# A two-layer block on one core: the gate rows spread by one fp32r product over high and low parts, and the first level of a block inverse built by VectorE's transpose on four quarters

## What is computed

```python
gc = jnp.cumsum(g, -1)
diff = gc[..., :, None] - gc[..., None, :]
decay = jnp.where(lower, jnp.exp(jnp.where(lower, diff, 0.0)), 0.0)
kb = k * beta[..., None]
L = jnp.where(strict, jnp.einsum('bhnid,bhnjd->bhnij', kb, k) * decay, 0.0)
rhs = jnp.concatenate([v * beta[..., None], kb * jnp.exp(gc)[..., None]], -1)
sol = lax.linalg.triangular_solve(L + jnp.eye(C, dtype=L.dtype), rhs, left_side=True,
                                  lower=True, unit_diagonal=True)
u, w = sol[..., :dv], sol[..., dv:]
```

## Time and profile before

| what | value |
|---|---|
| median of 3 runs | 2718.54 us (2718.34 to 2718.98) |
| profiled execution, span from first to last instruction | 2717.0 us |
| TensorE busy | 2678.4 us, 99% of the span |
| VectorE busy | 1909.8 us, 70% |
| ScalarE busy | 1212.6 us, 45% |
| GpSimd busy | 854.2 us, 31% |
| mean granted TensorE clock | 0.996 of full speed |

### The profile page before, as it was taken

The page is one execution under the profiler, slowest core; times in us unless marked ns, Lnnn a source line. Parts: engine busy times, 40 slices in busy tenths (PEclk is TensorE's granted clock), DMA queues, the critical chain, the costliest instruction groups (busy, mean ns, idle before and its releaser), DMA issues.

```text
span 2717.0 us, 45293 instructions
## 1 busy us (share of the span) xinstructions
PE 2678.4 (99%) x17387; PEld 2250.4 (83%) x17387; DVE 1909.8 (70%) x2190; ACT 1212.6 (45%) x1572; POOL 854.2 (31%) x646
## 2 busy tenths in 40 slices
PE   6999999999999999999999999999999999999998
PEld 4798998899898888888888888889777778888887
DVE  1476777787787687666666666588999997655554
ACT  2355455545546445333333333354433334444344
POOL 1076676676667412600000000004565550000000
PEclk9999999999999999999999999999999999999999
DMA  9966666676665676666666666655555556666664
GB/s 364 354 219 207 227 225 204 223 239 200 224 229 188 219 223 228 189 187 186 187 190 188 190 186 186 185 162 172 171 179 170 161 173 187 192 186 186 192 202 155
DMA packets 283976, 552.53 MB, mean 203 GB/s; under 512 B 16882, under 2 KB 54323, under 8 KB 282675
## 3 DMA queue, kind: packets, MB, share of 16 engines
q1 hardware_dynamic: 263488, 473.49, 56.5%
q0 software_dynamic: 19472, 76.06, 7.4%
q10 hardware_dynamic: 866, 0.80, 0.1%
HBM read 548.19 MB, written 2.10 MB: 203 GB/s over the span
## 4 chain that ended last, share of the span: by engine, by line
PE 96%; DMA 2%; DVE 1%; SPq 1%; ACT 0%; issue 0%; DVEq 0%
PE pg L1220 40%; PE pd L1220 18%; PE pg L936 13%; PE pg L923 6%; PE pg L1207 4%; PE pg L955 3%; PE pd L849 2%; DMA wr<-in_gdn_w_in 1%; PE pd L1096 1%; PE pd L1078 1%; PE pd L1415 1%; PE pd L1428 1%; DMA arena<-in_mod_w 1%; PE pg L849 1%; PE pd L1027 1%; PE pd L1010 1%
## 5 line engine op out<-in xcount | busy, mean ns | idle before, releaser
L2341 DVE TENSOR_TENSOR wl<-wr,wh 128x1024 fp32r<-128x1024 f32 x615 | 773.7, 1268 | 453.7 <-ACT wh L1818 451.2
L1818 ACT ACTIVATE wh<-wr 128x1024 fp32r<-128x1024 f32 x616 | 652.8, 1061 | 936.2 <-PE pg L1220 590.3
L662 POOL TENSOR_TENSOR wl<-wr,wh 128x1024 fp32r<-128x1024 f32 x195 | 478.9, 2458 | 366.3 <-ACT wh L1599 231.3
L1220 PE MATMUL pg<-wh,hh 128*128 128x512 f32 x1344 | 529.8, 394 | 0.3 <-DVE hl L2414 0.3
L1220 PE MATMUL pg<-wl,hh 128*128 128x512 f32 x1344 | 527.3, 392 | 0.0
L1220 PE MATMUL pg<-wh,hl 128*128 128x512 f32 x1344 | 525.7, 391 | 0.0
L1599 ACT ACTIVATE wh<-wr 128x1024 fp32r<-128x1024 f32 x216 | 227.7, 1057 | 356.4 <-PE pg L936 196.4
L1220 PEld LDWEIGHTS pg<-wh,hh 128*128 128x128 f32 x1344 | 252.6, 188 | 59.1 <-DVE wl L2341 2.4
L936 PE MATMUL pg<-hh,wh 128*128 128x256 f32 x1024 | 300.7, 294 | 0.8 <-ACT arena L1659 0.8
L1220 PEld LDWEIGHTS pg<-wh,hl 128*128 128x128 f32 x1344 | 252.5, 188 | 56.3
L1220 PEld LDWEIGHTS pg<-wl,hh 128*128 128x128 f32 x1344 | 252.3, 188 | 53.9
(11 more groups left out here) (446 smaller groups left out, 4727.3 us busy)
## 6 DMA issues: line engine op xcount, KB each, us to landing
wr<-in_w_in SPq DMA_DIRECT2D x224, 512.0 KB, 3.8
wr<-in_ffn_w_gu SPq DMA_DIRECT2D x176, 512.0 KB, 3.8
wr<-in_gdn_w_in SPq DMA_DIRECT2D x128, 512.0 KB, 4.1
arena<-in_mod_w POOLq DMA_DIRECT2D x60, 1024.0 KB, 6.7
wr<-in_ffn_w_down SPq DMA_DIRECT2D x88, 512.0 KB, 4.6
arena<-in_mod_w SPq DMA_DIRECT2D x32, 1024.0 KB, 13.7
wr<-in_gdn_w_in SPq DMA_DIRECT2D x128, 256.0 KB, 3.1
wr<-in_gdn_w_out SPq DMA_DIRECT2D x56, 512.0 KB, 4.5
```

The lines of the kernel that those rows point to most:

```text
L662: nc.gpsimd.tensor_tensor(wl[c % RING][:], wraw[c % 4], wh[c % RING][:].bitcast(F32), ALU.subtract)\
L1220: m = nc.tensor.matmul(halves(bank)[:, h, :], act[x][:, k0 + k, h * P:(h + 1) * P], w[s][:, k, :], skip_group_check=True, start=(first and ...
L1818: a(wh[c % 4][:], wraw[c % 4], ACT.Copy).then_inc(s_hc, 1)
L2341: v.tensor_tensor(wl[c % 4][:], wraw[c % 4], wh[c % 4][:].bitcast(F32), ALU.subtract).then_inc(s_lc, 1)
```

## The change

Three parts. First, the running gate sums are split once, in the setup, into a high and a low fp32r part (gparts, on 128 partitions: high and low of the two token halves); GpSimd multiplies all four with a pick matrix (pick4 in place of pick2) into an fp32r rowm of 128 partitions, and the step "rows" is two fp32r matmuls over 64 rows each in place of two fp32 matmuls over 32 rows.

Second, the flips leave TensorE. VectorE writes the masked first factor to Us, subtracts it from the identity there, and its transpose operation gives Tc. The step "t2" becomes "vt1" and holds only the four transposes of v; ScalarE's copy vtok waits for it and not for VectorE.

Third, the u step of level 2 takes the crossed order of the later levels: of its sixteen blocks those in their own half are read from Us, and the others from Uc, into which ScalarE copies two quarters of 64x256 ("u1"). The x step of level 2 is crossed too.

```diff
@@ -48,12 +48,12 @@
     return {n: i + 1 for i, n in enumerate(names)}
 
 
-PEO = order("ssq", "rows", "gram", "ktok", "t2", "x2", "tx2", "u2", "x4", "tx4", "u4", "x8",
+PEO = order("ssq", "rows", "gram", "ktok", "vt1", "x2", "tx2", "u2", "x4", "tx4", "u4", "x8",
             "tx8", "u8", "x16", "tx16", "u16", "x32", "tx32", "u32", "x64", "ux64", "v0", "md0", "s", "o0", "r",
             "qs", "v1", "o1", "md1")
-VO = order("qn", "qkn", "dt", "lt", "lm", "at", "tc", "uc", *[f"{a}{s}" for s in LEVELS for a in ("x", "t")],
+VO = order("qn", "qkn", "dt", "lt", "lm", "at", "us1", "tc", *[f"{a}{s}" for s in LEVELS for a in ("x", "t")],
            "x64", "u64", "md0", "o0", "rhs1", "o1", "oz", "md1", "on", "og")
-AO = order("rnq", "rn", "exp", "kg", "vtok", "z", *[f"u{s}" for s in LEVELS], "v0", "s", "qs", "v1", "qkv", "rstd")
+AO = order("rnq", "rn", "exp", "kg", "vtok", "u1", "z", *[f"u{s}" for s in LEVELS], "v0", "s", "qs", "v1", "qkv", "rstd")
 GO = order("rowm")
 
 
@@ -115,7 +115,7 @@
 AO0 = 1
 N_CST = 1 + 4 + 1 + 1 + 6
 A0 = {"cond": 1, "vec": 3, "x0": 4, "x3": 7, "sp": 9, "eb": 10, "decay": 12, "tok": 15}
-V0 = {"cw": 1, "gc": 2, "beta": 3}
+V0 = {"cw": 1, "gc": 2, "gparts": 3, "beta": 4}
 LATE_LOWS = (0, 1, 2, 4, 6)
 LATE_HALVES = (0, 3, 5, 7, 9, 11, 12, 13)
 MOD_SEQ = [c + 4 * i for c in range(4) for i in range(2)]
@@ -222,6 +222,7 @@
         Tb = take(8, P)
         Xc = Xb.rearrange("p a b -> p (a b)")[:, 0:512].rearrange("p (n t) -> p n t", t=64)
         Ub = take(8, P)
+        Us = Ub[:, :, 64:P]
         Tc, Uc = (Tb.rearrange("p a b -> p (a b)")[:, 512 * i:512 * (i + 1)].rearrange("p (n t) -> p n t", t=64)
                   for i in range(2))
         sqb = Xb.rearrange("p a b -> p (a b)")
@@ -237,9 +238,11 @@
         vn0 = take(VH, P)
         vn1, rhs1, ob, oz = kg0, vn0, dTb, lTb
         Sb = take(VH, P)
-        rowm = take(VH, P)
-        take(8)
-        take(VH * P - 8)
+        rowm_at = at[0]
+        take(VH, P)
+        gpart_at = at[0]
+        take(P)
+        take(VH * P - P)
         tk = take(7, NH)
         tkc = take(7, VH)
         cwc = take(4, 8)
@@ -690,9 +696,9 @@
 
             def batch(it, last=False):
                 restart()
-                rows = gcT[0:2 * NH, 0:P].unsqueeze(1).broadcast_to([2 * NH, VH, P])
-                pick = pick2[:, bass.ds(it * VH, VH)].unsqueeze(2).broadcast_to([2 * NH, VH, P])
-                nc.gpsimd.tensor_tensor(rowm[0:2 * NH], rows, pick, ALU.mult).then_inc(s_g, 1)
+                rows = gparts[:].bitcast(F32).unsqueeze(1).broadcast_to([P, VH, P])
+                pick = pick4[:, bass.ds(it * VH, VH)].unsqueeze(2).broadcast_to([P, VH, P])
+                nc.gpsimd.tensor_tensor(rowm[:], rows, pick, ALU.mult).then_inc(s_g, 1)
                 for t in range(1, 22):
                     if t == 5:
                         pool.wait_ge(s_v, it * len(VO) + VO["lm"])
@@ -1014,8 +1019,8 @@
                 pe.wait_ge(s_g, bg + GO["rowm"])
                 for n in range(2):
                     V(("qn", "qkn")[n])
-                    r = slice(NH * n, NH * (n + 1))
-                    m = nc.tensor.matmul(pd[0][:, n * 512:(n + 1) * 512], ones[r, :],
+                    r = slice(2 * NH * n, 2 * NH * (n + 1))
+                    m = nc.tensor.matmul(pd[0][:, n * 512:(n + 1) * 512], ones_r[r, :],
                                          rowm[r].rearrange("p a b -> p (a b)"), start=True, stop=True)
                 m.then_inc(s_pe, 1)
                 yield
@@ -1036,7 +1041,6 @@
                     m = tr(pd[0][:, 512 + h * P:512 + (h + 1) * P], vT[:, h, 0:P])
                 m.then_inc(s_pe, 1)
                 yield
-                V("lm")
                 Ac("kg")
 
                 def block(bank, half, i):
@@ -1044,22 +1048,20 @@
                     col = 512 * (i // 4) + 64 * (i % 4)
                     return bank[64 * half:64 * half + 64, col:col + 64]
 
-                def crossed(s, b, n):
-
-                    return (b, slot(n)) if s == 2 else (n % 2, 4 * b + n // 2)
+                def crossed(b, n):
+
+                    return n % 2, 4 * b + n // 2
+
+                def u_block(s, b, n):
+
+                    half, i = crossed(b, n)
+                    r = slice(64 * half, 64 * half + 64)
+                    return Us[r, n, :] if s == 2 and half == b else Uc[r, n // 2 if s == 2 else i, :]
 
                 def each_block():
                     for m in range(4):
                         yield from ((0, 2 * m), (1, 2 * m + 1), (0, 2 * m + 1), (1, 2 * m))
 
-                def flip_blocks(bank, src, at):
-                    for n in range(8):
-                        for b in range(2):
-                            r = slice(64 * b, 64 * b + 64)
-                            m = nc.tensor.matmul(block(bank, b, slot(n)), src[r, at(n), :], ident[r, r],
-                                                 start=True, stop=True)
-                    return m
-                flip_blocks(pd[0], Uc, slot)
                 for h in range(VH):
                     col = 512 * (h // 2) + 256 + P * (h % 2)
                     m = tr(pd[0][:, col:col + P], vT[:, h, P:T])
@@ -1075,7 +1077,7 @@
                     else:
                         for b, n in each_block():
                             r = slice(64 * b, 64 * b + 64)
-                            m = nc.tensor.matmul(block(pd[par], *crossed(s, b, n)), lTb[r, n, r], Tc[r, n, :],
+                            m = nc.tensor.matmul(block(pd[par], *crossed(b, n)), lTb[r, n, r], Tc[r, n, :],
                                                  start=True, stop=True)
                     m.then_inc(s_pe, 1)
                 V("at")
@@ -1084,16 +1086,12 @@
                 yield
                 for s in LEVELS:
                     V(f"x{s}")
-                    if s > 2:
-                        Ac(f"u{s // 2}")
-                    else:
-                        V("uc")
-                        Ac("vtok")
+                    Ac(f"u{s // 2}")
                     par ^= 1
                     for b, n in each_block():
-                        half, i = crossed(s, b, n)
+                        half, i = crossed(b, n)
                         r = slice(64 * half, 64 * half + 64)
-                        m = nc.tensor.matmul(block(pd[par], b, slot(n)), Uc[r, i, :], Xc[r, i, :], start=True, stop=True)
+                        m = nc.tensor.matmul(block(pd[par], b, slot(n)), u_block(s, b, n), Xc[r, i, :], start=True, stop=True)
                     m.then_inc(s_pe, 1)
                     yield
                     V(f"t{s}")
@@ -1700,9 +1698,12 @@
                     a(kg0[:, h, :], pd[0][:, (h // 2) * P:(h // 2 + 1) * P], ACT.Copy, scale=tkc[:, 6, h:h + 1])
                 a(vtok[:, 0:VH, :].rearrange("p a b -> p (a b)"), pd[0][:, 512:1024], ACT.Copy).then_inc(s_a, 1)
                 yield
-                V("tc")
+                PEw("vt1")
                 a(vtok[:, VH:8, :].rearrange("p (a b) t -> p a (b t)", a=2),
                   pd[0][:].rearrange("p (a c) -> p a c", a=2)[:, :, 256:512], ACT.Copy).then_inc(s_a, 1)
+                V("us1")
+                a(Uc[0:64, 0:4, :], heads(Us)[64:P, :, 0, :], ACT.Copy)
+                a(Uc[64:P, 0:4, :], heads(Us)[0:64, :, 1, :], ACT.Copy).then_inc(s_a, 1)
                 yield
                 silu_z(it)
                 yield
@@ -2130,8 +2131,8 @@
             v.tensor_copy(m1t[64:P, 0:64], m1t[64:P, 64:P])
             v.tensor_copy(identc[0:64], ident[0:64, 0:64])
             v.tensor_copy(identc[64:P], ident[64:P, 64:P])
-            for n in range(2):
-                v.tensor_copy(pick2[NH * n:NH * (n + 1)], ident[NH * n:NH * (n + 1), NH * n:NH * (n + 1)])
+            for n in range(4):
+                v.tensor_copy(pick4[NH * n:NH * (n + 1)], ident[NH * n:NH * (n + 1), NH * n:NH * (n + 1)])
             link(v.tensor_copy(masks[64:P, 0:5, 0:64], masks[64:P, 0:5, 64:P]))
             mod_column(1)
             for c in range(4):
@@ -2179,9 +2180,16 @@
             for c in range(TT):
                 link(v.tensor_tensor_scan(gx[0:NH, 3, c * P:(c + 1) * P], gx[0:NH, 0, c * P:(c + 1) * P],
                                           gx[0:NH, 1, c * P:(c + 1) * P], 0.0, ALU.mult, ALU.add))
-            v.tensor_copy(gx[NH:2 * NH, 3, 0:P], gx[0:NH, 3, P:T])
             v.tensor_scalar(gx[0:NH, 0, 0:P], gx[0:NH, 3, 0:P], -1.0, gx[0:NH, 3, P - 1:P], ALU.mult, ALU.add)\
                 .then_inc(s_v0, 1)
+            for c in range(TT):
+                m = v.tensor_copy(gparts[2 * NH * c:2 * NH * c + NH], gx[0:NH, 3, c * P:(c + 1) * P])
+            link(m)
+            for c in range(TT):
+                at0 = 2 * NH * c
+                m = v.tensor_tensor(gparts[at0 + NH:at0 + 2 * NH], gx[0:NH, 3, c * P:(c + 1) * P],
+                                    gparts[at0:at0 + NH].bitcast(F32), ALU.subtract)
+            m.then_inc(s_v0, 1)
             dve.wait_ge(s_a0, A0["eb"])
```

(19 more changed lines are left out.)

## The result

The changed kernel takes 2722.6 us, median of 21 runs (2720.8 to 2727.3), against 2718.5 for the kernel before (2718.1 to 2719.3): ratio 1.0013, 95% interval 1.0008 to 1.0019. It is a little slower, as forecast, but by 4.1 us, where 16.8 were predicted.

The account below looks back on a forecast made before the run. TensorE was taken to bound the kernel (busy 2678.4 of 2717.0 us). Waits of 5.35 less 2.75 saved give +2.6 an iteration; 7 x 2.6 = +18.2, less 1.4, is +16.8 on 2718.5: 2735.3 us, range 2698 to 2746.

Parts of the forecast that it names:

- what TensorE saves: Delta-rule iteration: flips and transposes 1.23, level 2 x and u steps 0.92, rows 0.60; 2.75 us saved per iteration.
- The 0.46 for the rows: Row product: two fp32r products one after the other take 0.46 us instead of 1.06, a gain of 0.60.
- that VectorE can't follow: Delta-rule iteration: VectorE's lead shrinks, halves meet low parts, and TensorE waits 5.35 us per iteration for its results.
- heavier: Rival, VectorE's transpose: it waits for low part 8 (2.19 us), an iteration costs +4.2, 2746.5 us in all; chance 0.12.
- the order at one meeting: GpSimd's low part 9 waits for VectorE's half 2 and runs to 280.8; low part 10 then splits half 3.
- the rest of its chain: After that meeting, low parts split later halves; TensorE waits 1.45, 0.2, 1.8, 0.5 and 1.4 us.
- the ends: Iterations 0 to 6 cost +2.6 us each, the first included; the last takes half the gain, -1.4.
- even: Rival: only the first wait and one of 1.4 to 1.8 come, 2.9 against 2.75; within 5 us of 2718.5; chance 0.10.
- The order holds: Rival: half 3 goes whole, an iteration gains 1.5 to 2.4 us, 2699 to 2707; chance 0.30 together with no waits.

Follow-up runs that it names:

- the best version: Changed kernel with modulation halves and GpSimd's DMA issues one step later, and one last-iteration output split later (LATE_LOWS 5 for 4): 2700.4 us (0.9941).
- The rows alone: Kernel before with only the gate rows as one fp32r product over high and low parts (rowm, gparts): 2713.6 us (0.9984).
- the order of the prediction forced: Changed kernel with GpSimd's low part 9 held by a semaphore until VectorE's modulation half 2 is done: 2748.1 us (1.0105).
- halves one step later: Changed kernel with modulation halves 2 to 15 one VectorE step later, DMA issues left in place: 2780.3 us (1.023).

## Why the prediction was right and wrong

**Right: what TensorE saves.** The predicted 2.75 us an iteration is what the best version shows (96.58 - 93.83); rows 0.45, the four transposes 0.44 and the x and u steps 0.62 each are as they were taken. The rows alone gave 4.8 us, 8 x 0.60. The 0.46 for the rows is right by luck: it was taken as two products one after the other, and the records have them side by side (last section).

**Right: that VectorE can't follow**, where it starts from, and that the wait is for results of VectorE behind halves that met a low part. The transpose takes 0.71 us, in all eight iterations, also where it lies wholly under a low part (279.64 to 280.35 under 279.01 to 281.87). The Trainium skill ("SBUF — State Buffer", Who interferes with whom) says that a VectorE operation with at most one SBUF input, outside the two-port modes, does not contend with GpSimd; the trace of this transpose agrees, and the rival "heavier" falls.

**Wrong: the order at one meeting**, "Low part 9, ready at 278.03 behind its DMA issue (0.80), waits for half 2". I let the operation that is recorded first have the port. Low part 9 is recorded 0.17 us after half 2's second operation and had it all the same. With the order of the prediction forced, the rest of its chain came about, wait for wait (1.9, 1.6, 0.8, 1.2 against 1.45, 1.8, 0.5, 1.4, and 0.2 predicted at the u step of level 4). Its total did not: 2748.1 us against the 2735.3 of the sum, so even with this order the sum is 13 us short, and the clock below is part of that. With low part 9 first, low part 10 meets half 3 at its first operation, half 4 is free, and one wait of 2.0 us takes the place of five with 5.35.

Why low part 9 won is shown as far as this: with the same neighbours and a smaller lead for VectorE it loses, if a semaphore keeps it back until VectorE's first operation is done. My reading is that GpSimd's next operation stands in line for the port while GpSimd still issues the transfer, so that it is served at the end of VectorE's first operation; that place in line itself is not in any row.

**The account of the 4.1 us.** By iterations: the first lost 4.5 us, the third 0.8, the other five up to the seventh gained 0.5 each, and from the start of the last (835.08, before 832.14) to the end 1.2 were lost. By causes: saved 8 x 2.75 = 22.0; waits 21.2, against 1.6 before: 19.6. That leaves -2.4, and 6.5 us are missing. Most of them are TensorE's clock. Windows of the changed kernel (stretch, its length, busy times, granted clock, share of DMA, GB/s), in iteration 2 and in the last:

```profile
384.00:388.00 4.00, 4.00 (x24) 4.00 (x22) 3.47 (x5) 0.15 (x1) 0.84 (x2) 0.57 0.89 264
...
872.00:877.00 5.00, 5.00 (x37) 3.87 (x39) 3.74 (x4) 0.61 (x1) 0.61 (x1) 0.66 0.50 148
```

In both the granted clock is near the lower of its two levels, 1.2 GHz, for some three microseconds, right behind a wait of 2.0 and 2.2 us; the same between 188 and 199 us, behind the wait of 2.4 us in the first iteration (0.84). Were TensorE at work all through them, they would cost 4 x 0.43, 5 x 0.34 and 11 x 0.16, some 1.7 us each, 5.2 together. In iteration 2, where the chunk behind the wait took 4.57 us for 3.06, the iteration is 1.3 longer than its neighbours (97.40 against 96.09); three times that is 3.9. The five other waits of 2.0 us had no such stretch behind them. The steps directly behind a wait are longer too: u2 0.69 for 0.62, the transposes 0.63 for 0.44, up to 0.26 us an iteration, some 2 us in all. With the stretches that makes 6 to 7.3, and the 6.5 lie between. This term, the clock, is not in my sum at all.

**Wrong in size: the ends.** The first iteration went by the predicted pattern (waits of 2.4, 1.6, 0.8 and 1.2) and cost 4.5 us and not 2.6, most of the difference being the clock. For the last I took half the gain, -1.4, and it cost 1.2; there TensorE waited 2.2 us behind VectorE's splits of outputs (L2313), with the clock at its lower level behind that.

Of the rivals "even" came nearest: it had 2718.5 within 5 us, from two waits of 2.9 us together in place of five, and the kernel has one of 2.0; but it has no clock in it either. "The order holds" did not come about. Half 3 was not split, as it has it (3.00 us, with low part 10 over its first operation alone), but half 2 was, and the reasons it gave are absent: the transpose took 0.71, and low part 10 was ready at 285.60, where 280.9 in the times of before makes 285.5. That the best version lies in its range of 2699 to 2707 does not bear it out, since that is another kernel.

## What to carry to other kernels

Before a microsecond is taken from the engine that bounds, look at the lead of the engine that feeds it: here 2 us of lead paid for the rows alone (0.6 us) and not for all three parts (2.75). Where two engines share a port and meet many times in an iteration, the moves have to be tried in pairs: one list moved by a step cost 58 us, both lists moved by a step gained 20, with the same work. And in such a chain, which of two operations goes first is not read from their recorded starts.

## What the runs showed of the hardware that was not expected

A GpSimd operation that follows a DMA issue of GpSimd without a gap went ahead of a VectorE operation recorded 0.17 us (changed kernel) and 0.59 us (halves one step later) before it. Held by a semaphore, the same operation lost with 0.07 us between them. It is no rule for all work without a gap: in the changed kernel low part 8 stands directly behind low part 7 and let the subtraction through, which was recorded 1.15 us before it.

Two fp32r products of 512 columns over 64 rows each, in different halves of the array, took 0.45 us of the chain, twice the 0.23 of one product over 128 rows. Yet they are not recorded one behind the other: both records lie in the same half microsecond (the profile models the ends of matmuls), and each lasts 0.50, where a product over 128 rows is recorded with 0.39. Why side by side gains nothing here is not shown.

```profile
262.79 0.50 PE L1023 MATMUL pd<-rowm,ones 64*128 64x512 f32 x2
```

A wait of TensorE of 2.0 us was followed by some three microseconds at the lower clock in one iteration (384 us) and by none in five others with the same wait.
